# A fused three-layer transformer kernel: the forget decay of one attention reaches the scores by transfers and an added bias, not by a picking matmul

## What is computed

```python
def fox_attention(xn, w_in, b_f, w_o):
    proj = xn @ w_in                      # q, k, v: 1024 wide each, and 16 forget logits
    log_f = jax.nn.log_sigmoid(f_logit.astype(jnp.float32))
    cum = jnp.cumsum(log_f, axis=1)       # per head, along the tokens
    o = causal_block_attention(q, k, v, 1.0 / math.sqrt(FOX_HEAD_DIM), cum)
    return o.reshape(B, S, FOX_WIDTH) @ w_o
```

## Time and profile before

| | |
|---|---|
| median of 3 runs | 1012.64 us (1012.0 to 1012.66) |
| the profiled execution's own time | 1011.0 us |
| its span | 1009.3 us |
| TensorE busy / weight loads | 992.8 us (98%) / 921.0 us (91%) |
| VectorE busy | 714.1 us (71%) |
| ScalarE busy | 609.4 us (60%) |
| GpSimd busy | 52.8 us (5%) |
| granted TensorE clock | 0.998 of full |
| slab loads | 512 KB each, 4.1 us from issue to landing in the median |

### The profile page before, as it was taken

One profiled execution on the slowest core, in us unless ns is written; L12 is line 12 of the kernel. 1 busy time (PEld: TensorE's weight loads), 2 busy tenths in 40 slices (PEclk: granted clock), 3 DMA queues, 4 the chain that ended last, 5 costly groups with the idle time before them and its releaser, 6 DMA issues.

```text
span 1009.3 us, 19691 instructions
## 1 busy us (share of the span) xinstructions
PE 992.8 (98%) x7190; PEld 921.0 (91%) x7190; DVE 714.1 (71%) x1359; ACT 609.4 (60%) x1092; POOL 52.8 (5%) x69
## 2 busy tenths in 40 slices
PE   7999999999999999999999999999999999999997
PEld 7999899999999999999999999999999989999996
DVE  5567987776666668666496666668878586666665
ACT  6577785575555556565475555557668675555553
POOL 3011000120000002000020000002200020000000
PEclk9999999999999999999999999999999999999999
DMA  9643445465565554434445665564666456565531
GB/s 349 216 145 127 135 154 180 149 206 184 178 186 184 186 184 162 155 125 131 163 149 187 186 187 187 187 187 139 191 193 195 141 166 188 187 187 187 187 125 43
DMA packets 50696, 174.05 MB, mean 172 GB/s; under 512 B 6096, under 2 KB 8656, under 8 KB 50512
## 3 DMA queue, kind: packets, MB, share of 16 engines
q1 hardware_dynamic: 49456, 172.12, 52.8%
q10 hardware_dynamic: 1184, 1.18, 0.6%
HBM read 169.86 MB, written 1.05 MB: 169 GB/s over the span
## 4 chain that ended last, share of the span: by engine, by line
PE 89%; DVE 7%; ACT 2%; DMA 1%; issue 1%; SPq 0%; DVEq 0%; ACTq 0%
PE bank L396 87%; DVE w_lo L1399 2%; PE bank L586 1%; DVE a_pair L1418 1%; DVE xT L1429 1%; DVE arena_r L1418 1%; DMA xT<-xT_dram 0%; DVE arena L1392 0%; SPq L370 0%; DMA tmp<-arena 0%; DVE tmp L1392 0%; DVE arena_r L1399 0%; ACT a_pair L1000 0%; DVE arena L1714 0%; ACT w_hi L949 0%
## 5 line engine op out<-in xcount | busy, mean ns | idle before, releaser
L396 PE MATMUL bank<-a_pair,w_hi 128*128 128x256 f32 (+1 forms) x1992 | 539.9, 343 | 7.5 <-ACT a_pair L1210 7.1
L396 PE MATMUL bank<-a_pair,w_lo 128*128 128x256 f32 x1488 | 418.1, 282 | 0.0
L1399 DVE TENSOR_TENSOR w_lo<-stage,w_hi 128x1024 fp32r<-128x1024 f32 (+1 forms) x320 | 387.1, 1218 | 11.2 <-ACT w_hi L949 9.7
L396 PEld LDWEIGHTS bank<-a_pair,w_hi 128*128 128x128 f32 x1992 | 344.5, 191 | 53.5 <-DVE w_lo L1399 8.8
L396 PE MATMUL bank<-arena_r,w_hi 128*128 128x256 f32 x1792 | 329.0, 284 | 1.0 <-DVE arena_r L1399 0.5
L396 PEld LDWEIGHTS bank<-arena_r,w_hi 128*128 128x128 f32 x1792 | 278.3, 191 | 6.4 <-DVE arena_r L1399 1.5
L396 PEld LDWEIGHTS bank<-a_pair,w_lo 128*128 128x128 f32 x1488 | 283.7, 191 | 0.0
L396 PE MATMUL bank<-arena_r,w_lo 128*128 128x256 f32 x896 | 252.7, 283 | 0.0
L949 ACT ACTIVATE w_hi<-stage 128x1024 fp32r<-128x1024 f32 x194 | 204.8, 1056 | 35.6 <-PE bank L396 33.1
L965 ACT ACTIVATE w_hi<-stage 128x1024 fp32r<-128x1024 f32 (+2 forms) x126 | 127.9, 1027 | 77.2 <-PE bank L396 69.8
L396 PEld LDWEIGHTS bank<-arena_r,w_lo 128*128 128x128 f32 x896 | 171.0, 191 | 0.0
(11 more groups left out here) (170 smaller groups left out, 657.2 us busy)
## 6 DMA issues: line engine op xcount, KB each, us to landing
stage<-slab_dram SPq DMA_DIRECT2D x319, 512.0 KB, 4.1
con<-con_dram SPq DMA_DIRECT2D x1, 1153.5 KB, 10.9
xT<-xT_dram SPq DMA_DIRECT2D x4, 256.0 KB, 5.3
arena<-arena ACTq DMA_DIRECT2D x1, 1024.0 KB, 8.7
arena<-tmp SPq DMA_DIRECT2D x32, 32.0 KB, 3.8
out_dram<-arena SPq DMA_DIRECT2D x3, 256.0 KB, 2.5
tmp<-arena SPq DMA_DIRECT2D x16, 16.0 KB
vec<-vec_dram SPq DMA_DIRECT2D x1, 245.5 KB, 3.8
```

The costliest lines, as they stand in the source:

```text
L396: return nc.tensor.matmul(out, lhsT, rhs, start=start, stop=True, skip_group_check=True)
L1399: return nc.vector.tensor_tensor(out, a, hi.bitcast(f32), ALU.subtract)
```

## The change

`decay` becomes a tile of 128 partitions by 16 heads by 256 keys. The 16 rows go from PSUM to `o_raw` by one copy of ScalarE, from there to a tensor in memory (`decay_dram`), and from there each pair of rows comes back, read by all 128 partitions. GpSimd adds the causal mask to it, head by head, into one of four bias tiles (in `tmp`). `maxima` adds that bias where it added the mask. The product with `pick` goes, the product with the triangle is made once and without the extra columns, and the first four pairs stand one step later in `FOX_AT`.

```diff
-FOX_AT = {FOX + s: k for k, s in enumerate((6, 8, 10, 12, 15, 17, 21, 23))}
+FOX_AT = {FOX + s: k for k, s in enumerate((7, 9, 11, 13, 15, 17, 21, 23))}
...
-        pick = sb("pick", [P, HEADS], f32r)
-        decay = span(arena_r, 6144, 384)
+        decay = chunks(arena, 6144, 16)
+        decay_rows = o_raw[0:HEADS, 0, :]
+        rows_d = nc.dram_tensor("decay_dram", (HEADS, TOK), f32, kind="Internal").ap()
+        bias = tmp[:, :, :].rearrange("p c t -> p (c t)").rearrange("p (i n) -> p i n", i=4)
...
+            def decay_out(k):
+
+                if k == 0:
+                    sp.wait_ge(rows_ready, 1)
+                    sp.dma_start(rows_d, decay_rows).then_inc(rows_out_done, 16)
+                    sp.wait_ge(rows_out_done, 16)
+                sp.dma_start(decay[:, 2 * k:2 * k + 2, :],
+                             rows_d[2 * k:2 * k + 2, :].unsqueeze(0).to_broadcast([P, 2, TOK])).then_inc(decay_in[k], 16)
+
...
             for n in range(FOX, FOXO):
                 load(n, n + {1: 1, 2: -1}.get((n - FOX) % 6, 0))
+                if FOX + 15 <= n < FOX + 23:
+                    decay_out(n - FOX - 15)
...
                 for out, of_q, of_k in TILES:
                     for b, g, r in heads:
-                        mm(b[:, out], fox_q[r, k, of_q], fox_k[r, k, of_k], out.start == 0)
-                for b, g, r in heads:
-                    r = slice(r.start, r.start + 48)
-                    mm(b[:, 0:384], pick[r, g:g + 1].to_broadcast([48, P]), decay[r, :], False).then_inc(s_done, 1)
+                        last = mm(b[:, out], fox_q[r, k, of_q], fox_k[r, k, of_k], out.start == 0)
+                        if out.start:
+                            last.then_inc(s_done, 1)
...
                         pe.wait_ge(f_ready, 1)
-                        for r in (0, 64):
-                            out = bank[7][r:r + 16, 256:512]
-                            mm(bank[7][r:r + 16, 128:256], forget[:, 64:80], con[:, C_TRIF:C_TRIF + P], True)
-                            mm(out, forget[:, 64:80], con[:, C_TRIF:C_TRIF + TOK], True)
-                            last = mm(out[:, P:TOK], forget[:, 80:96], con[:, C_TRIF:C_TRIF + P], False)
-                        last.then_inc(c_done, 1)
+                        out = bank[7][0:HEADS, TOK:2 * TOK]
+                        mm(out, forget[:, 64:80], con[:, C_TRIF:C_TRIF + TOK], True)
+                        mm(out[:, P:TOK], forget[:, 80:96], con[:, C_TRIF:C_TRIF + P], False).then_inc(c_done, 1)
...
-                    act.wait_ge(pick_ready, 4)
-                    for r in (0, 64):
-                        last = nc.scalar.activation(decay[r:r + 16, :], bank[7][r:r + 16, 128:512], ACT.Copy)
-                    last.then_inc(chi_ready, 1)
+                    nc.scalar.activation(decay_rows, bank[7][0:HEADS, TOK:2 * TOK], ACT.Copy).then_inc(rows_ready, 1)
...
-                i = 2 * (g % 2)
+                i, mask = 2 * (g % 2), span(con, C_MCAUSAL, 384)
+                if g < HEADS:
+                    dve.wait_ge(bias_ready, g + 1)
+                    mask = bias[:, g % 4, :]
...
-                if n == FOX + 5:
-                    dve.wait_ge(chi_ready, 1)
-                    for a in (0, 64):
-                        minus_hi(decay[a + 32:a + 48, :], bank[7][a:a + 16, 128:512], decay[a:a + 16, :]
-                                 ).then_inc(decay_ready, 1)
...
+                if m == 2:
+                    for g in range(HEADS):
+                        pool.wait_ge(decay_in[g // 2], 16)
+                        if g >= 4:
+                            pool.wait_ge(s_taken, g - 3)
+                        for cols, keys in ((slice(0, P), slice(0, P)), (slice(P, 384), slice(0, TOK))):
+                            last = nc.gpsimd.tensor_tensor(bias[:, g % 4, cols], decay[:, g, keys],
+                                                           con[:, C_MCAUSAL + cols.start:C_MCAUSAL + cols.stop], ALU.add)
+                        last.then_inc(bias_ready, 1)
```

More of the change, by code:

```diff
@@ L197, in trunk @@
                              "fflo_ready"))
-        wf_ready, wfhi_ready, f_done, f_abs, f_log, f_ready, c_done, pick_ready, chi_ready, decay_ready = (
-            sem(n) for n in ("wf_ready", "wfhi_ready", "f_done", "f_abs", "f_log", "f_ready", "c_done", "pick_ready",
-                             "chi_ready", "decay_ready"))
+        wf_ready, wfhi_ready, f_done, f_abs, f_log, f_ready, c_done, rows_ready, bias_ready = (
+            sem(n) for n in ("wf_ready", "wfhi_ready", "f_done", "f_abs", "f_log", "f_ready", "c_done",
+                             "rows_ready", "bias_ready"))
+        decay_in = [sem(f"decay_in{i}") for i in range(8)]
         s_done, s_taken, p_exp, p_ready, t_done, t_taken, o_done, o_hi, o_lo = (
@@ L214, in trunk @@
         silu_scaled = sem("silu_scaled")
-        pick_clear, f_raw, f_turned = sem("pick_clear"), sem("f_raw"), sem("f_turned")
+        f_raw, f_turned = sem("f_raw"), sem("f_turned")
+        rows_out_done = sem("rows_out_done")
         swap_clear, sine_signed = sem("swap_clear"), sem("sine_signed")
@@ L613, in fox_scores @@
                 pe.wait_ge(qk_taken, 16 + 2 * (k + 1))
-                pe.wait_ge(decay_ready, 2)
                 if k:
@@ L1481, in masked_max @@
                 return nc.vector.tensor_tensor_reduce(
-                    out=s[:, cols], in0=b[:, cols], in1=con[:, mask + cols.start:mask + cols.stop], scale=1.0,
+                    out=s[:, cols], in0=b[:, cols], in1=mask[:, cols], scale=1.0,
                     scalar=-3.0e38, op0=ALU.add, op1=ALU.max, accum_out=s_max[:, i:i + 1])
@@ L1492, in da_max @@
                     for t, cols in enumerate(TILES):
-                        last = masked_max(2 * e + t, bank[6 + e], C_MCHUNK, soft_s[:, e, :], cols)
+                        last = masked_max(2 * e + t, bank[6 + e], span(con, C_MCHUNK, 384), soft_s[:, e, :], cols)
                 chain(last)
@@ L1526, in maxima @@
                     dve.wait_ge(p_exp, g - 1)
-                i = 2 * (g % 2)
+                i, mask = 2 * (g % 2), span(con, C_MCAUSAL, 384)
+                if g < HEADS:
+                    dve.wait_ge(bias_ready, g + 1)
+                    mask = bias[:, g % 4, :]
                 for t, cols in enumerate(TILES):
-                    last = masked_max(i + t, soft_bank(g), C_MCAUSAL, soft_s[:, g % 2, :], cols)
+                    last = masked_max(i + t, soft_bank(g), mask, soft_s[:, g % 2, :], cols)
                 chain(last)
```

## The result

| | before | after |
|---|---|---|
| median of 20 runs each | 1011.81 us (1011.09 to 1012.82) | 1016.17 us (1010.41 to 1017.76) |
| ratio | | 1.0037, 95% interval 1.0031 to 1.0043 |
| the profiled execution: own time, span | 1011.0, 1009.3 us | 1015.89, 1014.1 us |
| GpSimd busy | 52.8 us | 66.3 us |

The change makes the kernel slower by 0.37%. The forecast was 1011.3 us, at most 1013.5, worked out from a median of 1012.64 before: 0.13% faster.

The account below looks back on a forecast made before the run. TensorE was taken to bound the kernel, busy 105.00 of 105.00 us in the changed attention; -1.65 us there plus a 0.3 us stall made about -1.35, from 1012.64 to 1011.3 us, range 1010.5 to 1013.5.

Parts of the forecast that it names:

- TensorE's sum, -1.65 us: TensorE in the changed attention: picking products gone -1.36 us, triangle -0.5, new places +0.2, in all -1.65 us.
- The scores block: TensorE's block of scores for a pair of heads: without picking products 0.86 us instead of 1.03, 8 pairs, 1.36 us gained.
- the triangle: TensorE's triangle product, made once without extra columns: 0.5 us gained of 1.21, between 0.4 and 0.75.
- the places: First four pairs one step later in TensorE's order of blocks: a loss of 0.2 us.
- The mechanism: First pair's transpose on TensorE: a bias later than 416.7 us stalls it us for us; expected at 416.95, stall 0.3.
- The slab loads: SyncE's loads of later slabs: stay hidden behind a cover of some 8 us, costing TensorE nothing.
- the later pairs: Pairs after the first: their bias comes easier, with reads and GpSimd ahead, so no stall at their transposes.
- "At least 2.0, at most 2.5" for the write: Write of the 16 KB of decay rows to memory: bounded by larger transfers' times, taken as 2.1 us.
- "At most 3.3" for the read: Read of 256 KB by all partitions: at least 2.0 us, at most 3.3 from a slab twice its size; taken as 2.5.
- GpSimd and VectorE, 0.25 us on `probs`: Rival, chance 0.06: the engines hold each other up, `probs` stretches, 0.25 us on one to five pairs; 1011.5 to 1012.6.
- The late-bias rival: Rival, chance 0.17: TensorE waits 1 to 3.6 us at the first transpose; with all upper bounds, stall 2.6, 1013.6 us.
- The slower rival: Rival, chance 0.07: the read by 128 partitions takes up to 7.9 us, bias at 422.35, stall 5.7, 1016.7 us.

## Why the prediction was wrong

- **TensorE's sum, -1.65 us**: right. The scores block came out at 0.86 us, the triangle gained 0.46 us where 0.5 was taken, and the places cost 0.06 where 0.2 was taken; the traces give 1.8 in all, and without the decay the kernel gains 2.2 (1.3 to 3.1).
- **The mechanism**, a bias in time or a stall at the first transpose us for us: right in place. The slab loads and the later pairs cost nothing, as said.
- **"At least 2.0, at most 2.5" for the write**: failed at both ends. 1.4 us when nothing meets it, 2.55 to 3.5 when an instruction packet does. Bounds from larger transfers hold neither a collision nor the small size. The fixed cost of about 2 us that the Trainium skill's page *DMA: Bandwidth & Descriptors*, "Latency and other measured facts", gives lies between the two.
- **"At most 3.3" for the read**: failed. 3.1 to 3.4 us alone, and SyncE's next slab load, which the prediction had seen behind it and costed only for the slab's sake, makes it about 4.2.
- **GpSimd and VectorE, 0.25 us on `probs`, as a rival of its own**: the size was off, 0.57 us, and 1.1 with the small instructions and head 1's bias. And it was no rival: a late bias puts GpSimd's next additions just beside `probs`, so the two come together. The Trainium skill's rule named there (*GPSIMD Engine Reference*, "Specifications") fits the low part, which has two SBUF inputs and went from 1.22 to 1.75. `probs` reads one SBUF tile and doubled too (0.55 to 1.12); that fits the rule only if it ran in the 2-port mode, which no run shows.
- **No term for the clock**: the step that was missing. The late-bias rival took a stall of 2.6 us to cost 2.6. The 3.9 us cost 5.6, and the range's upper end lacked this.
- The slower rival was to decide from a bias later than 420.4. The bias came at 420.16, and the loss was reached by the longer chain behind it and the clock; the read took 4.2 us, not over 5.9.

## What to carry to other kernels

A wait of a few us of a TensorE that is otherwise full can cost more than its length: here waits of 3.3 to 4.1 us were followed by a loss of 1.4 to 2.8 more at half clock, and waits of up to 1.0 us by none. When a chain of small steps through memory must meet a full engine, sum its upper bounds with what its own lateness brings beside it, and leave room, or take other traffic out of its way: one slab later, or one copy first, turned +0.37% into -0.18% and -0.11%. Where a small transfer takes 1.4 us in one profile and 3.1 in another, look at which packet it meets.

## What the runs showed of the hardware

- The 16 KB instruction packet near the write takes 0.88 to 1.24 us of one DMA engine. A transfer of 16 rows whose last 1 KB stands behind it lands 1.1 to 1.25 us after it, while undisturbed it lands 0.4 us after the last row has started. Why that tail is 0.7 to 0.85 us longer is open.
- A read of 2 KB by all 128 partitions (256 KB) takes 3.1 to 3.4 us alone, about as long as a slab of 512 KB.
- For equal idle times of 3.8 us the half clock lasted 2.7 and 5.9 us. What sets this is open.
